# Expert weight stream of a two-block transformer kernel: plan order, places in SBUF, and the order of TensorE's steps

## What is computed

```python
x = layer_norm(DEEPNORM_ALPHA * x + mix, ln_mix_g[i], ln_mix_b[i])
ple = (p[i] @ ple_w_proj[i]) * jax.nn.sigmoid(x @ ple_w_gate[i])
ffn = grouped_moe(x, router_w, router_bias, moe_w1[i], moe_w3[i], moe_w2[i])
x = layer_norm(DEEPNORM_ALPHA * x + ffn + ple, ln_ffn_g[i], ln_ffn_b[i])
```

## Time and profile before

| what | value |
|---|---|
| median of 3 runs | 1251.97 us (1249.4 to 1252.17) |
| the profiled execution's own time | 1248.62 us |
| its span in the profile | 1246.8 us |
| granted TensorE clock, mean | 0.992 of full speed |
| TensorE busy | 1204.7 us, 97% |
| VectorE busy | 648.3 us, 52% |
| ScalarE busy | 509.4 us, 41% |
| HBM read | 336 MB, 270 GB/s over the span |

### The profile page before, as it was taken

One profiled execution on the slowest core, in us unless ns is written; L12 is line 12 of the kernel. 1 busy time (PEld: TensorE's weight loads), 2 busy tenths in 40 slices (PEclk: granted clock), 3 DMA queues, 4 the chain that ended last, 5 costly groups with the idle time before them and its releaser, 6 DMA issues.

```text
span 1246.8 us, 16795 instructions
## 1 busy us (share of the span) xinstructions
PE 1204.7 (97%) x6900; PEld 842.2 (68%) x6900; DVE 648.3 (52%) x943; ACT 509.4 (41%) x750; POOL 206.3 (17%) x207
## 2 busy tenths in 40 slices
PE   6999999999999999999999999998999999999995
PEld 5888888887688888888873434334898774444331
DVE  7666657856876887648761111105667772111103
ACT  5665455647466455424531111115578531111112
POOL 0000000230499993012000000000033100000000
PEclk9999999999999999989999999999999999999998
DMA  9555554541455555424889999999533499999994
GB/s 391 202 198 185 187 203 138 200 169 69 177 175 197 197 178 199 177 78 141 332 326 426 428 426 426 427 425 389 200 117 129 189 412 419 426 427 427 427 426 185
DMA packets 49330, 338.23 MB, mean 271 GB/s; under 512 B 5473, under 2 KB 5473, under 8 KB 10465
## 3 DMA queue, kind: packets, MB, share of 16 engines
q1 hardware_dynamic: 47520, 330.54, 67.4%
q10 hardware_dynamic: 1728, 6.55, 1.3%
HBM read 336.02 MB, written 1.05 MB: 270 GB/s over the span
## 4 chain that ended last, share of the span: by engine, by line
PE 85%; DMA 5%; DVE 5%; ACT 3%; issue 1%; SPq 0%; DVEq 0%; ACTq 0%
PE pb L180 84%; DMA ring<-in_moe_w 2%; DMA extra<-in_moe_w 2%; DVE halves L310 1%; ACT halves L302 1%; DMA ring<-in_ffn_w 1%; DVE XTb L410 1%; PE pb L2220 0%; DVE XTb L404 0%; DVE XN L363 0%; DVE XN L352 0%; DVE Xs L420 0%; ACT Xs L1674 0%; DVE SM L1591 0%; DVE Xs L1659 0%
## 5 line engine op out<-in xcount | busy, mean ns | idle before, releaser
L180 PE MATMUL pb<-XTb,halves 128*128 128x256 f32 (+1 forms) x2080 | 332.5, 320 | 4.5 <-DVE XTb L410 3.4
L310 DVE TENSOR_TENSOR halves<-ring,halves 128x2048 fp32r<-128x2048 f32 (+1 forms) x120 | 280.0, 2355 | 91.4 <-ACT halves L302 91.4
L180 PEld LDWEIGHTS pb<-XTb,halves 128*128 128x128 f32 x2080 | 299.5, 190 | 39.1 <-issue 3.1
L302 ACT CAST halves<-ring 128x2048 fp32r<-128x2048 f32 (+1 forms) x122 | 226.8, 1875 | 47.0 <-PE pb L180 44.7
L180 PE MATMUL pb<-halves,XTb 128*128 128x512 f32 x768 | 181.0, 394 | 3.0 <-DVE XTb L1714 1.7
L180 PEld LDWEIGHTS pb<-halves,XTb 128*128 128x128 f32 x768 | 143.5, 189 | 34.5 <-DVE halves L310 1.6
L180 PE MATMUL pb<-ring,gather 128*64 128x512 f32 x608 | 138.0, 596 | 0.0
L2357 DVE TENSOR_TENSOR slots_h<-slots_silu,pb 128x256 f32<-128x256 f32 x32 | 13.5, 421 | 224.7 <-ACT slots_silu L2317 224.7
L180 PE MATMUL pb<-halves,HTh 128*128 128x512 f32 x352 | 109.0, 391 | 0.0
L180 PEld LDWEIGHTS pb<-ring,gather 128*64 128x64 f32 x608 | 42.0, 137 | 78.5 <-issue 78.0
L180 PE MATMUL pb<-extra,gather 128*64 128x512 f32 x416 | 94.6, 597 | 0.0
(11 more groups left out here) (372 smaller groups left out, 1382.4 us busy)
## 6 DMA issues: line engine op xcount, KB each, us to landing
ring<-in_moe_w SPq DMA_DIRECT2D x122, 1024.0 KB, 15.3
ring<-in_ffn_w SPq DMA_DIRECT2D x66, 1024.0 KB, 4.8
extra<-in_moe_w SPq DMA_DIRECT2D x62, 1024.0 KB, 15.6
ring<-in_w_tok SPq DMA_DIRECT2D x10, 1024.0 KB, 4.8
ring<-in_ple_gate SPq DMA_DIRECT2D x8, 1024.0 KB, 4.8
extra<-in_moe_w SPq DMA_DIRECT2D x12, 512.0 KB, 26.0
ring<-in_w_out SPq DMA_DIRECT2D x4, 1024.0 KB, 4.8
ring<-in_ab_out SPq DMA_DIRECT2D x4, 1024.0 KB, 4.8
```

The costliest lines, as they stand in the source:

```text
L180: return e.matmul(out, l, r, start=start, stop=stop, **kw)
L302: e.copy(split_of(n)[0], raw_of(n)).then_inc(*high.mark(n))
L310: e.tensor_tensor(l, raw_of(n), h.bitcast(F32), ALU.subtract).then_inc(*low.mark(n))
```

## The change

1. **Plan order.** After `p` and `ple_proj` come expert blocks 0 and 1, then gate blocks 0 to 2, expert blocks 2, 4, 5, gate block 3, then expert block 3 and all from 6 on.
2. **Places.** The extra places grow from 6 to 8: one at `rest` used once in a layer (ONCE), one in two parts used once (PARTED); the first six expert blocks have fixed homes (FIRST_HOMES). `p`, `ple_proj` and the gate blocks (`narrow`) take their high part from 3 split places, not 4, so that the fourth is open to an expert block.
3. **Sigmoid in place.** The gate's sigmoid stays in PSUM, so the first gather into a bank waits for VectorE's product (`ple_mul`), not for the sigmoid. VectorE does two products, then two sums.
4. **TensorE's half step.** `turn` writes to bank 5 + n, and `gather` comes ahead of `turn` and `up(p, n, 1)` (but for the first one).
5. **Norm vectors.** Those after the experts of layer 0 are asked for at the start of layer 1's mixer, those after layer 1's at p = 8, once the last weights have landed.
6. The dense path's buffers (not taken in these runs) move, small values shrink from 704 to 480 columns.

```diff
-EXTRA = 6
+EXTRA = 8
...
+        E0 = RING + SPLIT
+        ONCE, PARTED = E0 + 6, E0 + 7
+        FIRST_HOMES = {0: E0 + 4, 1: E0 + 5, 2: PARTED, 3: ONCE, 4: E0 + 2, 5: E0 + 3}
...
+            plan_one(("p", i), a["p"][i])
+            plan_all(("ple_proj", i), a["ple_proj"][i])
+            plan_experts((0, 1))
+            for g in range(3):
+                plan_one((("ple_gate", i), g), a["ple_gate"][i, g])
+            plan_experts((2, 4, 5))
+            plan_one((("ple_gate", i), 3), a["ple_gate"][i, 3])
+            plan_experts((3, *range(6, 96)))
...
+            if n in at_layer:
+                i = at_layer[n]
+                done, most = (index["sb_out", 3], index["sb_out", 1]) if i else (index["w_glu"], index["w_glu"])
+                latest[E0:E0 + 2] = [index[("ple_gate", i), 3]] * 2
+                latest[E0 + 2:E0 + 4] = [most] * 2
+                if i == 0:
+                    latest[E0 + 4:E0 + 6] = [index["w_out", 3]] * 2
+                latest[ONCE:] = [done, most]
+            at = first_home.get(n)
+            if at is None:
+                at = min(range(E0 + EXTRA if n in whole else RING), key=lambda s: latest[s])
             home.append(at)
             gone.append(latest[at])
-            latest[at] = n
-            landings[at] += 1
+            latest[at] = n if at < ONCE else len(plan)
+            landings[at] += 2 if at == PARTED else 1
             landed.append(16 * landings[at])
-            at = min(range(RING, RING + SPLIT), key=lambda s: latest[s])
+            at = min(range(RING, RING + SPLIT - (n in narrow)), key=lambda s: latest[s])
...
             for q, b in enumerate((0, 1, 3, 2)):
-                e.wait_ge(*ple_gate.at(i, b))
+                e.wait_ge(*ple_mul.at(i, b))
...
-                e.activation(gate_sig[:, b * 512:b * 512 + 512], banks[4 + b][:, :], ACT.Sigmoid)...
+                e.activation(banks[4 + b][:, :], banks[4 + b][:, :], ACT.Sigmoid)...
...
                 if half == 0 and p:
-                    e.wait_ge(*s.mul.at(p - 1, n))
+                    e.wait_ge(*s.h_kept.at(p - 1, n))
...
             def turn(p, n):
                 e.wait_ge(*s.mul.at(p, n))
-                if p < 6:
-                    e.wait_ge(*s.x_kept.at(p // 2 + 1, 2 * (p % 2) + n))
-                else:
-                    e.wait_ge(*s.h_kept.at(p - 1 + n, 1 - n))
                 for c in range(2):
-                    j = e.transpose(banks[7]...
+                    j = e.transpose(banks[5 + n]...
...
             def gather(p, n):
+                dp, q = p // 2 + 1, 2 * (p % 2) + n
                 if n or p:
-                    e.wait_ge(*s.h_kept.at(p - 1 + n, 1 - n))
+                    e.wait_ge(*s.x_kept.at(dp - (q == 0), (q + 3) % 4))
...
+                    if p < 6 and p + n:
+                        gather(p, n)
                     if n == 1 and p < 8:
                         turn(p, 0)
...
-                    if p < 6:
+                    if p + n == 0:
                         gather(p, n)
...
+                    if p == 8 and n == 0 and i:
+                        e.wait_ge(*s.gathered.at(3, 3))
+                        e.wait_ge(land_second[3], 32)
+                        act_norm_load(e, 3)
...
-                if p == 6:
-                    e.wait_ge(*s.gathered.at(3, 3))
-                    act_norm_load(e, 2 * i + 1)
...
                 if i:
                     act_xt_affine(e, c)
+                    act_norm_load(e, 1)
                     act_stick(e, c)
```

More of the change, by code:

```diff
@@ L188, in both @@
             return [f(y) for y in x]
-        plan, index, whole = [], {}, set()
+        plan, index, whole, first_home = [], {}, set(), {}
+        E0 = RING + SPLIT
+        ONCE, PARTED = E0 + 6, E0 + 7
+        FIRST_HOMES = {0: E0 + 4, 1: E0 + 5, 2: PARTED, 3: ONCE, 4: E0 + 2, 5: E0 + 3}
         def plan_one(key, src):
@@ L233, in build @@
                 plan_all("sb_out", a["sb_out"])
[L234 to L237, removed]
+            experts_in_order = []
             for p in range(9):
@@ L242, in build, with plan_experts @@
                             for x in (2 * p, 2 * p + 1):
-                                plan_one((("moe", i), "w13", x, n, half), a["moe_w13"][i, x, n, half])
+                                experts_in_order.append(((("moe", i), "w13", x, n, half), a["moe_w13"][i, x, n, half]))
                     if p:
                         for x in (2 * p - 2, 2 * p - 1):
-                            plan_one((("moe", i), "w2", x, n), a["moe_w2"][i, x, n])
-            whole.update(range(first, len(plan)))
+                            experts_in_order.append(((("moe", i), "w2", x, n), a["moe_w2"][i, x, n]))
+            def plan_experts(numbers):
+                for k in numbers:
+                    first_home[len(plan)] = FIRST_HOMES.get(k)
+                    whole.add(len(plan))
+                    plan_one(*experts_in_order[k])
+            plan_one(("p", i), a["p"][i])
[6 more added lines that the diff above has]
+            plan_experts((3, *range(6, 96)))
         in_halves = {index[("moe", i), "w2", x, h]: 2 * h + x - 14 for i in range(2) for h in range(2) for x in (14, 15)}
         land_second = [sem(f"land_second{i}") for i in range(4)]
+        narrow = {index[key] for i in range(2) for key in [("p", i), (("ple_proj", i), 0)] + [(("ple_gate", i), g) for g in range(4)]}
+        at_layer = {index["p", i]: i for i in range(2)}
         home, high_home, gone, high_gone, landed = [], [], [], [], []
@@ L275, in build @@
         high, low, used = signal("w_high"), signal("w_low"), signal("w_used")
-        extra = [place(f"extra{i}", at, SCOLS) for i, at in enumerate((xt_at, xt_at + 2048, rest + 11520, rest + 13568, rest + 15744, rest + 17792))]
+        extra = [place(f"extra{i}", at, SCOLS) for i, at in enumerate((xt_at, xt_at + 2048, rest + 11520, rest + 13568, rest + 15872, rest + 17920, rest))]
+        parted = [place(f"parted{i}", at, 1024) for i, at in enumerate((rest + 10496, pr_at + po["bre"][0]))]
         def place_of(x, s, n):
@@ L321, in whole_weights @@
             e.wait_ge(land[home[n]], landed[n])
-            return n, raw_of(n).rearrange("p (k n) -> p k n", k=4)
+            if home[n] == PARTED:
+                return n, [parted[k // 2][:, k % 2 * 512:k % 2 * 512 + 512] for k in range(4)]
+            return n, [raw_of(n)[:, k * 512:k * 512 + 512] for k in range(4)]
         def sp_stream(e):
@@ L333, in sp_stream @@
                             e.dma_start(raw_of(m)[:, 1024:2048], plan[m][:, 1024:2048]).then_inc(land_second[in_halves[m]], 16)
+                    continue
+                if home[n] == PARTED:
+                    for k in range(2):
+                        e.dma_start(parted[k], src[:, k * 1024:k * 1024 + 1024]).then_inc(land[home[n]], 16)
                     continue
@@ L2141, in dve_before_moe @@
             e.wait_ge(*ple_kept.at(i))
[L2142 to L2148, removed]
+            for pair in ((0, 1), (3, 2)):
+                for b in pair:
+                    dst = ple[:, b * 512:b * 512 + 512]
+                    e.wait_ge(*ple_gate.at(i, b))
+                    e.tensor_tensor(dst, dst, banks[4 + b][:, :], ALU.mult).then_inc(*ple_mul.mark(i, b))
+                for b in pair:
+                    x = X3[:, b // 2, (b % 2) * 512:(b % 2) * 512 + 512]
+                    e.wait_ge(*ple_mul.at(i, b))
+                    e.scalar_tensor_tensor(x, x, ALPHA, ple[:, b * 512:b * 512 + 512], ALU.mult,
+                                           ALU.add).then_inc(*ple_added.mark(i, b))
             e.wait_ge(*slot_gates.at(i))
@@ L2498, in dve_dense @@
                     e.wait_ge(*f.mul.now())
-                    e.wait_ge(*f.gates.at(p))
+                    e.wait_ge(*f.gates.at(p if p == 0 else 7))
                     if n == 0 and p >= 2:
```

30 lines of the change are left out of this document (13 added, 17 removed).

## The result

The changed kernel takes 1294.32 us (median of 4 runs, 1293.53 to 1295.96) against 1252.07 us (4 runs, 1249.4 to 1253.5): ratio 1.0344, 95% interval 1.033 to 1.0359. It is slower by 42.3 us; the forecast was 48.3 us slower, 1300.3. The profiled execution took 1295.03 us, its span is 1293.1 us.

The account below looks back on a forecast made before the run. TensorE and the weight stream arrive together, the later deciding each expert stage. Terms 14.0 + 8.1 + 14.4 + 11.8 = 48.3 us on the median 1251.97 gave 1300.3 us; 8-in-10 range 1278 to 1316.

Parts of the forecast that it names:

- Part 1, the stream: Expert stages: SyncE held at the twelfth expert block until block 0 is used; +14.0 us in layer 0, +14.4 in layer 1.
- about 617: Sign of being right: SyncE issues no expert request between about 617 and 660, restarting as TensorE ends its first expert step.
- the restart: Expert stages: starting the stream from an empty queue costs 2.3 us more, bounds 0 to 4.8.
- Part 2, the casts: Ahead of the norms: high-part casts wait for three split places, delaying VectorE's chain; +8.1 us in layer 0, +11.8 in layer 1.
- the second order effect by `p`: Layer 1: `p`'s cast waits for `sb_out` 1, so exponentials and `pe_finish` come 2.3 us later.
- Part 3, the half step: TensorE's expert steps: eleven breaks fewer per layer, 2.2 to 3.3 us, counted as 0 since the stream covers it.
- A break's price: Gather between up and down: 0.2 us for a break, up to 0.3 with up's last matmul.
- Parts 4 and 5: Sigmoid in place and later norm vectors: nothing each; the vectors' block is left out of the stream's sum.
- Faster because the places fall otherwise: Rival: twelfth block and `ple_proj`'s high part get places that free early; 1244.6 us, 5 in 100.
- Only the hold: Rival: only SyncE's hold bites, the casts being covered; +28.4, 1280.4 us, 10 in 100.
- only the casts: Rival: the stream keeps up; +19.9 us with TensorE's 7.4 saved, 1264.5 us, 5 in 100.
- The clock: Rival: last 12 us of each expert stage at half speed after new pauses; +24, 1324 us, 8 in 100.

Follow-up runs that it names:

- The half step alone: Kernel before with the new half step only (gather ahead of turn, turn into bank 5 + n): 1250.7 us, ratio 1.0002.
- with the vectors: Kernel before with the new half step and the late norm vectors: 1245.3 us, ratio 0.9955; again 1245.0 us, ratio 0.9948.
- Repairing the rule alone: Changed kernel with the next block's place chosen by time of use, not plan number: 1264.5 us, ratio 1.0100.
- the repaired kernel: Changed kernel with places chosen by use and four split places for p and ple_proj: 1243.0 us, ratio 0.9927; again 1241.9 us, ratio 0.9937.
- the pairs of kernels: Late against early norm vectors: kernel before with new half step, 1245.3 and 1250.7 us; changed kernel with both places edits, 1243.0 and 1248.9 us.
- kernels with one of the two costs: Changed kernel with four split places for p and ple_proj, 1275.9 us (1.0189); changed kernel with places chosen by use, 1264.5 us (1.0100).

## Why the prediction was right

**What bounds the kernel.** Right: TensorE and the stream end together. The half step alone (1.0002) and with the vectors (0.9955) show that before the change the stream decided by a hair.

**Part 1, the stream.** Right in mechanism: the twelfth block waits for block 0, 11 blocks have landed, and the queues stand empty, as the trace shows. Repairing the rule alone brought 29.8 us. The requests stop at 628.97 and not at about 617, because the last two of the eleven wait until `p` and `ple_proj` have been used, which the casts delay; all eleven land well before block 0 is used, so the sum isn't touched. The sizes were 12.6 and 12.0 us, not 14.0 and 14.4. In layer 0, at 423 GB/s over 202.6 us, the stream moved 81.7 blocks, where I had 82.0; at 2.46 us each that is 201.0, so the restart cost 1.6 us where I took 2.3 from a lone block's landing. In layer 1 it moved 81.7 where I had 82.2, at 2.467 us each 201.5, so the restart cost 1.0 us there. Half a block and 1.3 us of restart are the 2.4 us by which layer 1 came out smaller, within the rounding of the rates. The 2.3 us came from comparing a lone block's landing with a block's share of a full stream; that part of it which every block pays, full stream or not, I had counted as restart (argued, not tried).

**Part 2, the casts.** Right in both places, the second order effect by `p` among them: `pe_finish` starts at 999.75 in the changed kernel, 1.6 us of it waiting for ScalarE's exponentials. 8.9 and 11.0 us against 8.1 and 11.8: the sum of the two is exact only by luck, for two things that I didn't have offset each other. In layer 0 the casts cost 8.1 us as said, and a fallen clock behind them 0.8 more (below). In layer 1 the first addition comes 11.7 us late (1013.77 against 978.34, less the 23.8 by which all is late there), but VectorE's last step ahead of the router (L434, L404 before) only 11.0 (1025.99 against 991.24): in the kernel before it waited 1.24 us for ScalarE there, now 0.56.

**Part 3, the half step.** Hidden in the change, as said. A break's price was a little undersized: 0.36 us by the half step's period (13.10 and 12.74), not 0.2 to 0.3. By the starts in the two timelines the gather is 0.21 us shorter (8 matmuls in 0.94 us, 707.67 to 708.61, against 1.15) and the up ahead of it, or now ahead of the down, 0.10 (3.48 against 3.58), both as I had them; the down behind is 0.04 shorter (3.44 against 3.48), which I hadn't.

**Parts 4 and 5.** The sigmoid in place cost nothing, as far as the repaired kernel shows; it wasn't tried alone. The vectors I counted as one block each, in the stream's sum; the pairs of kernels give 2.7 to 3.5 us each, not clear of the 2.46.

**The sum** was too large by 6 us. The stream's terms were 3.8 us too large. The terms were made against the passages of one profiled execution, and by spans they hold nearly: 48.3 less 3.8, plus the 2.3 at the start, less 0.4 at the end is 46.4, and the spans differ by 46.3. The medians differ by 42.3, since the profiled execution before lay 3.5 us under its median of 1252.07 and the changed kernel's 0.7 over its own. The costs also don't add up exactly: alone in the repaired kernel the casts are 21.5 us (1264.5 - 1243.0) and the hold 32.9 (1275.9 - 1243.0), 54.4 together, and both at once 51.3; with intervals of some 2 us on each ratio the 3 us between them aren't clear of noise.

**The rivals.** Faster because the places fall otherwise: the mechanism was true, its condition false. Repaired, the kernel takes 1241.9 to 1243.0 where that rival said 1244.6. Only the hold, and only the casts: neither alone, but kernels with one of the two costs take 1275.9 and 1264.5, where these rivals said 1280.4 and 1264.5. The clock: it did fall after the new pauses, but not in the starved stage.

## What to carry to other kernels

When requests are issued in order by one queue, a place must be chosen by when its occupant will be used, not by where it stands in the list; the moment a list stops being in order of use, a rule that sorts by number turns early prefetches into a lock on everything behind them. Before pricing what an edit saves on the busiest engine, ask how many blocks the stream has in hand: the same half step was worth nothing in one kernel and 7 us in the other. And a staging place taken from a chain of casts costs nothing only if the block that frees it is used before the cast is due.

## What the runs showed of the hardware

**The clock.** In both layers TensorE has two long pauses ahead of the router: 3.71 us (ahead of 613.77 and 1014.60) and, after some more work, 2.00 us (ahead of 624.00 and 1024.83). After the first the granted clock fell in both layers, at its lowest to 0.50, the lower level of 1.2 GHz, for 4 to 6 us. After the second it fell in layer 0 (0.59 and 0.56) and stayed at 1.00 in layer 1. Stretches of the changed kernel:
```profile
614.00:616.00 2.00, 2.00 (x6) 1.57 (x6) 1.90 (x5) 0.00 (x0) 0.00 (x0) 0.53 1.02 430
616.00:618.00 2.00, 2.00 (x7) 1.47 (x6) 1.96 (x4) 1.86 (x2) 0.00 (x0) 0.62 1.01 426
...
624.00:626.00 2.00, 2.00 (x10) 1.68 (x10) 1.45 (x3) 1.53 (x4) 0.00 (x0) 0.59 0.00 0
626.00:628.00 2.00, 2.00 (x7) 1.56 (x6) 2.00 (x4) 0.53 (x2) 0.00 (x0) 0.56 0.00 0
...
1014.00:1018.00 4.00, 3.40 (x8) 2.75 (x9) 3.86 (x7) 1.03 (x2) 0.00 (x0) 0.50 1.00 414
1018.00:1022.00 4.00, 3.76 (x13) 2.44 (x13) 3.90 (x8) 0.96 (x1) 0.00 (x0) 0.71 1.01 426
1022.00:1026.00 4.00, 1.99 (x17) 1.52 (x16) 3.34 (x8) 2.35 (x6) 0.00 (x0) 1.00 0.07 27
1026.00:1030.00 4.00, 4.00 (x31) 3.74 (x30) 4.00 (x5) 1.94 (x4) 0.00 (x0) 1.00 0.29 80
```
The work behind the first pause is in the shadow of the norm chain, so only the fall on the way to the router is paid, and it stands in layer 0 alone. VectorE's last step ahead of the router (L434) starts at 625.16, against 614.79 before: 8.1 us late, once the 2.3 of the start are taken off. Then the same six matmuls take 2.71 us in layer 0 and 1.64 in layer 1:
```profile
625.43 2.71 PE L180 MATMUL pb<-halves 128*128 128x512 f32 x6
...
1025.90 1.64 PE L180 MATMUL pb<-halves 128*128 128x512 f32 x6
```
That is where 8.1 us become 8.9. The Trainium skill (TensorE: Matmul & The Clock Gate, What's actually happening) has the half rate after idling. The rows behind both pauses of 3.71 us agree; of the two pauses of 2.00 us one was followed by a fall and one wasn't.

In the last part of the starved expert stage TensorE stood idle 12 to 13% of the time, in pauses of mostly 1.2 to 1.4 us, and its clock stayed at 1.00:
```profile
843.00:853.00 10.00, 8.78 (x42) 3.44 (x40) 0.42 (x1) 0.76 (x2) 0.00 (x0) 1.00 1.01 424
853.00:863.00 10.00, 8.71 (x40) 3.48 (x38) 0.75 (x1) 1.06 (x2) 0.00 (x0) 1.00 1.01 427
```
So a stage short of data in small, even portions cost the data's delay and nothing on top.

**Broadcast vectors.** Beside a full stream a megabyte of them took 2.56 us of the 16 DMA engines' time, where a block of weights took 2.49, by the packets of the two queues in the kernel before. In whole kernels, by two pairs that differ in them alone (1245.3 and 1250.7, 1243.0 and 1248.9), a megabyte of them is worth 2.7 to 3.0 us, with over 1 us of noise by my estimate.
